# Another order of work on ScalarE and VectorE around three norms and the PLE gate of an encoder layer

## Chip, cores and metric

The kernel runs on one core of a Trainium2 chip. The metric is the device time of one launch in microseconds (us); a lower number is better. The engines of the core are TensorE (PE), VectorE (DVE), ScalarE (ACT), GpSimd (POOL) and SyncE (SP, which issues most of the DMAs). Each engine takes its instructions strictly in the order of its program and waits on semaphores for the others.

## What is computed

One inference layer of a streaming encoder, for 512 prompt tokens and 64 sample tokens, handled together as 576 columns. Everything is float32. The parts that matter here:

```python
    merged = (jax.nn.sigmoid(gate_a) * (o_a.reshape(B, L, -1) @ w_branch_attn)
              + jax.nn.sigmoid(gate_r) * (o_r @ w_branch_ret))
    x = x + rmsnorm(merged @ w_out, g_mix_post)
    h = rmsnorm(x, g_ffn_pre)
    f = (jax.nn.silu(h @ w_ffn_gate) * (h @ w_ffn_up)) @ w_ffn_down
    x = x + rmsnorm(f, g_ffn_post)
    x = x + (p @ w_ple_proj) * jax.nn.sigmoid(x @ w_ple_gate)
```

`D_MODEL` is 1024, the FFN is 2816 wide, and the per-layer embedding `p` (PLE) has 256 columns. `rmsnorm` multiplies each token by the inverse root of its mean square over the 1024 features, then each feature by a gain. Attention and retention come earlier and are not touched.

## The kernel before

**Layout.** Activations lie transposed: features on the 128 partitions, tokens along the free axis. A tensor of width 1024 is eight blocks k (`KD` = 8) of 576 columns, and each block is handled as two halves h of 288 columns (`HALF`). So `(c, h)` names output block c of the features and half h of the tokens.

**Products in three passes.** A float32 operand is split into a high part (a copy rounded to fp32r, made by ScalarE) and a low part (the difference, made by VectorE). `triple` issues three matmuls for each input block k: high times high, high weight times low activation, low weight times high activation. So a unit of one `(c, h)` over eight blocks is 24 matmuls (`half_unit`); `several` runs two or four units side by side, k in the outer loop, so that the blocks of the activation may still be arriving. `hooks` and `behind` put small matmuls between them. On ScalarE `hi` splits a weight tile, on VectorE `lo` makes its low part; for the tiles of the last product both are called `gate_operand`. TensorE waits for a weight tile by a count in `lo_ready`.

**A norm.** It runs once for each half. ScalarE squares each block, VectorE adds the squares into `sqacc`. Then `half_sums_of` (TensorE, six narrow matmuls in the profile's records) sums over the partitions, `half_var_of` (VectorE) scales the sums, `half_power` (GpSimd, L2410) takes the power -0.5, and `half_factor` (TensorE, again six) spreads the factor over the partitions into PSUM.

**The first two norms.** After the product "out", norm 1 gives `scale` and `residual` (VectorE, new x in `res`). Its squares (`res_square` on ScalarE, `add_res_square` on VectorE) feed norm 2, whose factor goes into `normed`. `y_high` (ScalarE) and `y_low` (VectorE) split the result for the FFN. Half 0 goes through all this first, then half 1. The 16 units of "ple" (6 matmuls each, `ple_units`) give TensorE other work in the meantime, and `ple_tile` (ScalarE) copies each result out of PSUM. TensorE's order: ple blocks 0 to 5; "ffn" units 0 to 3 of half 0 side by side; ple blocks 6 and 7; ffn units 0 and 1 of half 1; ffn units 2 and 3 of half 1; ffn units 4 and 5. The first ScalarE function of the FFN is `gate_silu` (L1432).

**The FFN** is 19 groups of seven products and three rounds of "down". Its last round comes with norm 3: `down_out` (VectorE, L2216) adds the PSUM result to `wd`, `down_square` (ScalarE) squares it, `add_down_square` (VectorE) adds, and `scale`, `residual`, `y_high` and `y_low` follow as before, this time without a norm of their own. In this round a down unit has 7 input blocks, 21 matmuls. Order on TensorE: blocks 4 to 7 of half 0, then blocks 4 to 7 of half 1; the sums of half 0 stand in the middle of block 4 of half 1.

**The PLE gate.** Units 0 to 3 of "gate" run as four pairs (two for each half), then units 4 to 7 one by one. For each of the 16 results, in the order `Y_ORDER`: ScalarE applies the sigmoid (`gate_out`, L1568, in place 0 of the order the first use of that table here), VectorE multiplies and adds (L2275, L2277) into `yt`, TensorE transposes it back to rows (`y_transposes(n)`, L1095, three matmuls), ScalarE copies it (`y_rows_out`, L1576), and SyncE sends it out: one DMA for half 0, three for half 1, since half 1 holds rows of two output tensors. Result n on VectorE waits for the transposes of result n - 2.

**Lines of the page that recur.** L942, L943 and L944 are the three matmuls of `triple`, L995 the sums, L1003 the factor. L1918 is VectorE's `lo`, L1955 `scale`, L1964 `residual`, L1972 `normed`, L1978 `y_low`, L1991 `add_res_square`, L2224 `add_down_square`, L1899 VectorE's `gate_operand`. L1392 is `ple_tile`, L1386 `y_high`.

## Time and profile before

| | |
|---|---|
| median of 3 runs | 1001.41 us (1001.06 to 1001.5) |
| the profiled execution, its time | 1001.08 us |
| its span, first to last instruction | 999.2 us |
| TensorE busy | 978.2 us, 98% |
| VectorE busy | 632.1 us, 63% |
| ScalarE busy | 397.0 us, 40% |
| GpSimd busy | 85.7 us, 9% |
| mean granted clock of TensorE | 0.996 of full speed |

All times below are microseconds from the start of the span. A busy share is a mean over the whole span; the stretches around the norms have to be read by themselves. A timeline row gives start, duration, engine, line, operation, output and inputs, and in brackets how long the engine had been idle and what ended that.

### The profile page before, as it was taken

The page shows a single profiled execution, that of the slowest core. Times are in us where ns is not written, and L with a number is a line of the kernel's source. Part 1 is how long each engine was busy: PE and PEld are TensorE (multiplying, and loading weights), DVE is VectorE, ACT ScalarE, POOL GpSimd, SP SyncE. Part 2 cuts the span into 40 slices and gives each one's busy share as a digit, 9 for nine tenths or more (in the row PEclk, how much of TensorE's full clock was granted, in tenths as well). Part 3 has the DMA queues.
Part 4 walks back from the last instruction along what each step waited for, and adds up shares of the span by engine and source line. Part 5 has one row for each costly group of instructions (what it writes and reads, how often), then busy time and mean ns, then how long its engine had stood idle before and what let it go on. Part 6 is the DMA issues. An engine that isn't in the chain of part 4 may idle for free.

```text
span 999.2 us, 19155 instructions
## 1 busy us (share of the span) xinstructions
PE 978.2 (98%) x7256; PEld 954.8 (96%) x7256; DVE 632.1 (63%) x1244; ACT 397.0 (40%) x693; POOL 85.7 (9%) x140
## 2 busy tenths in 40 slices
PE   6999999999999999999998999999999999999997
PEld 5999999999999999999998999999999999999997
DVE  5555666757665634345466899625996469965762
ACT  5324434434343422223454555424453135533252
POOL 1032212212100000010011100000000000030000
PEclk9999999999999999999999999999999999999999
DMA  8434222122222222246512623521334223274211
GB/s 210 126 111 131 82 69 58 58 73 64 62 65 64 84 86 76 82 131 193 151 31 59 228 78 92 148 64 45 110 95 133 64 72 98 81 249 136 85 47 50
DMA packets 166198, 98.45 MB, mean 99 GB/s; under 512 B 14657, under 2 KB 162529, under 8 KB 165873
## 3 DMA queue, kind: packets, MB, share of 16 engines
q1 hardware_dynamic: 159904, 79.19, 28.0%
q0 software_dynamic: 4336, 16.67, 4.7%
q10 hardware_dynamic: 1888, 1.64, 0.6%
q8 instruction: 47, 0.77, 0.3%
q14 instruction: 23, 0.18, 0.1%
HBM read 86.79 MB, written 10.75 MB: 98 GB/s over the span
## 4 chain that ended last, share of the span: by engine, by line
PE 91%; DVE 4%; issue 2%; ACT 2%; DMA 0%; DVEq 0%; SPq 0%; ACTq 0%
PE acc L679 35%; PE acc L942 10%; PE acc L943 10%; PE acc L944 10%; PE small L942 6%; PE small L943 6%; PE small L944 6%; PE small L811 1%; PE small L828 1%; PE small L857 1%; PE small L861 1%; PE small L759 1%; PE small L859 1%; PE small L1095 1%; ACT prob L1183 1%
## 5 line engine op out<-in xcount | busy, mean ns | idle before, releaser
L679 PE MATMUL acc<-xh,whi 128*128 128x288 f32 x736 | 163.1, 303 | 1.6 <-DVE wlo L1606 1.5
L679 PE MATMUL acc<-xh,wlo 128*128 128x288 f32 x736 | 157.3, 295 | 0.0
L679 PE MATMUL acc<-xl,whi 128*128 128x288 f32 x736 | 157.2, 295 | 0.0
L1123 ACT ACTIVATE whi<-raw 128x1024 fp32r<-128x1024 f32 (+1 forms) x62 | 62.1, 1001 | 198.3 <-PE acc L679 198.3
L1606 DVE TENSOR_TENSOR wlo<-raw,whi 128x1024 fp32r<-128x1024 f32 (+1 forms) x64 | 74.2, 1160 | 81.1 <-ACT whi L1123 77.7
L679 PEld LDWEIGHTS acc<-xh,whi 128*128 128x128 f32 x736 | 116.9, 189 | 6.1 <-issue 5.0
L679 PEld LDWEIGHTS acc<-xl,whi 128*128 128x128 f32 x736 | 118.1, 188 | 0.0
L679 PEld LDWEIGHTS acc<-xh,wlo 128*128 128x128 f32 x736 | 118.0, 188 | 0.0
L1918 DVE TENSOR_TENSOR wlo<-raw,whi 128x512 fp32r<-128x512 f32 (+2 forms) x93 | 80.9, 871 | 51.1 <-ACT whi L1334 35.4
L942 PE MATMUL acc<-yh,whi 128*128 128x288 f32 x360 | 107.3, 298 | 1.3 <-DVE wlo L1918 1.3
L944 PE MATMUL acc<-yh,wlo 128*128 128x288 f32 x360 | 106.1, 295 | 0.0
L942 PE MATMUL acc<-fh,whi 128*128 128x288 f32 x264 | 78.3, 297 | 0.0
L944 PE MATMUL acc<-fh,wlo 128*128 128x288 f32 x264 | 78.3, 297 | 0.0
L943 PE MATMUL acc<-fl,whi 128*128 128x288 f32 x264 | 78.3, 296 | 0.0
L943 PE MATMUL acc<-yl,whi 128*128 128x288 f32 x264 | 77.7, 294 | 0.0
L1342 ACT ACTIVATE whi<-s_sum 128x512 fp32r<-128x512 f32 x76 | 47.7, 630 | 61.5 <-DVE s_sum L2100 51.4
L942 PEld LDWEIGHTS acc<-yh,whi 128*128 128x128 f32 x360 | 67.6, 188 | 1.7 <-DVE wlo L1918 1.5
L944 PEld LDWEIGHTS acc<-yh,wlo 128*128 128x128 f32 x360 | 67.6, 188 | 0.0
L1918 DVE TENSOR_TENSOR wlo<-s_sum,whi 128x512 fp32r<-128x512 f32 x76 | 51.6, 682 | 8.6 <-ACT whi L1342 8.6
L1334 ACT ACTIVATE whi<-raw 128x1024 fp32r<-128x1024 f32 (+1 forms) x38 | 38.4, 1012 | 39.6 <-PE acc L944 18.5
L944 PEld LDWEIGHTS acc<-fh,wlo 128*128 128x128 f32 x264 | 50.0, 189 | 0.0
L942 PEld LDWEIGHTS acc<-fh,whi 128*128 128x128 f32 x264 | 50.0, 189 | 0.0
(312 smaller groups left out, 2353.8 us busy)
## 6 DMA issues: line engine op xcount, KB each, us to landing
raw<-in_w_in SPq DMA_DIRECT2D x92, 256.0 KB, 3.1
raw<-in_w_ffn_gate SPq DMA_DIRECT2D x44, 256.0 KB, 3.3
raw<-in_w_ffn_up SPq DMA_DIRECT2D x44, 256.0 KB, 4.0
raw<-in_w_ffn_down SPq DMA_DIRECT2D x32, 256.0 KB, 3.5
res<-x_scratch POOLq DMA_DIRECT2D x16, 288.0 KB, 3.8
raw<-in_w_branch_ret SPq DMA_DIRECT2D x16, 256.0 KB, 3.1
raw<-in_w_out SPq DMA_DIRECT2D x16, 256.0 KB, 4.0
raw<-in_w_ffn_down SPq DMA_DIRECT2D x16, 192.0 KB, 3.7
```

The lines of the kernel that those rows point to most:

```text
L679: ins = nc.tensor.matmul(acc[:, a, hf, 0:HALF], w[:, s, at:at + P], x(k)[:, hf * HALF:(hf + 1) * HALF], start=first and n == 0 and m == 0, ...
L759: ins = nc.tensor.transpose(small[:, at + r * P:at + r * P + size], src[0:size, r, col:col + P], ident[0:size, 0:size])
L811: ins = nc.tensor.matmul(att[0:nq, slot * KW + k0:slot * KW + k1], q_st[64 * g:64 * g + 64, 2 * p + j, 0:nq], k_st[64 * g:64 * g + 64, k0: ...
L828: ins = nc.tensor.matmul(att[64 * g:64 * g + 64, 0:2 * nq], v_st[0:nk, t, 64 * g:64 * g + 64], prob_t[0:nk, t, 2 * g * nq:2 * (g + 1) * nq ...
L942: nc.tensor.matmul(bank, w_h, x_h, start=first, stop=False)
L943: nc.tensor.matmul(bank, w_h, x_l, start=False, stop=False)
L944: return nc.tensor.matmul(bank, w_l, x_h, start=False, stop=last)
L1123: nc.scalar.activation(whi[:, s, 0:n], raw[:, s, 0:n], ACT.Copy).then_inc(hi_ready, 1)
L1334: nc.scalar.activation(dst[:, 0:n], raw_of(RAW[u])[:, 0:n], ACT.Copy).then_inc(hi_ready, 1)
L1342: nc.scalar.activation(dst[:, 0:QUART], s_sum[:, S_STEP[u[2]], :], ACT.Copy).then_inc(hi_ready, 1)
L1606: nc.vector.tensor_tensor(wlo[:, s, 0:n], raw[:, s, 0:n], whi[:, s, 0:n].bitcast(F32), ALU.subtract).then_inc(lo_ready, 1)
L1918: nc.vector.tensor_tensor(dst[:, 0:n], src[:, 0:n], high[:, 0:n], ALU.subtract).then_inc(lo_ready, 1)
```

## The change

It has four parts.

- Norms 1 and 2. On VectorE, `lo` of the ffn weight tiles 1, 2 and 3 moves up, ahead of the loop of `normed` for half 0. On ScalarE the copies `y_high` of half 0 alternate with `ple_tile` from an earlier place on; the eight `res_square` of half 1 follow without `ple_tile` between them; the four `ple_tile` of blocks 6 and 7 move behind `gate_silu(0, 0)`; and a one-element Silu ahead of the squares asks for the table. On TensorE, the sums of half 1 move from behind ple unit (7, 0) to a hook after input block 6 of ffn units 0 to 3, and the factor moves from behind (7, 1) to behind (6, 0).
- Norm 3. `gate_operand(2)` goes behind the last square of half 0 on ScalarE and behind `half_var_of(0, 2)` on VectorE; `gate_operand(3)` goes behind `down_square(4, 1)` and behind `half_var_of(1, 2)`.
- The gate. A one-element Sigmoid on ScalarE stands ahead of the copies `y_high` of half 1. The transposes of results 0 to 3 move from hooks 5 (third pair) and 1, 3, 5 (fourth pair) to hooks 1, 3, 5, 7 of the fourth pair.
- The last two units of the gate are exchanged: (7, 1) runs before (7, 0).

```diff
--- before.py
+++ after.py
@@ -187,7 +187,7 @@
         c0 = KD * g
         order += both("down", range(c0, c0 + KD)) if g < 2 else \
             both("down", range(c0, c0 + 4)) + split("down", range(c0 + 4, c0 + KD))
-    return order + split("gate", range(4)) + both("gate", range(4, KD))
+    return order + split("gate", range(4)) + both("gate", range(4, KD - 1)) + [("gate", KD - 1, 1), ("gate", KD - 1, 0)]
 
 
 def use_order():
@@ -1023,7 +1023,7 @@
             pe.wait_ge(pl_ready, KP)
             behind = {(1, 1): lambda: half_sums_of(0, (sqr_added, 7)), (2, 1): lambda: half_sums_of(1, (sq_added, 14)),
                       (3, 0): lambda: half_factor(0, 1), (4, 1): lambda: half_factor(1, 0),
-                      (7, 0): lambda: half_sums_of(1, (sqr_added, 14)), (7, 1): lambda: half_factor(1, 1)}
+                      (6, 0): lambda: half_factor(1, 1)}
 
             def ple_units(cs):
 
@@ -1040,7 +1040,8 @@
                             behind[(c, h)]()
 
             ple_units(range(PLE_FIRST))
-            several("ffn", [(n, 0) for n in range(4)], yh, yl, ready=lambda k: pe.wait_ge(y_lo, k + 1))
+            several("ffn", [(n, 0) for n in range(4)], yh, yl, ready=lambda k: pe.wait_ge(y_lo, k + 1),
+                    hooks={6: lambda: half_sums_of(1, (sqr_added, 14))})
             ple_units(range(PLE_FIRST, KD))
             several("ffn", ((0, 1), (1, 1)), yh, yl, ready=lambda k: pe.wait_ge(y_lo, KD + k + 1))
             several("ffn", ((2, 1), (3, 1)), yh, yl)
@@ -1099,16 +1100,14 @@
             several("gate", ((0, 0), (1, 0)), yh, yl, ready=lambda k: pe.wait_ge(y_lo, 2 * KD + k + 1),
                     hooks={5: lambda: half_sums_of(1, (sq_added, 28))})
             several("gate", ((2, 0), (3, 0)), yh, yl, hooks={0: lambda: half_factor(1, 2)})
-            several("gate", ((0, 1), (1, 1)), yh, yl, ready=lambda k: pe.wait_ge(y_lo, 3 * KD + k + 1),
-                    hooks={5: lambda: y_transposes(0)})
-            several("gate", ((2, 1), (3, 1)), yh, yl, hooks={1: lambda: y_transposes(1), 3: lambda: y_transposes(2),
-                                                             5: lambda: y_transposes(3)})
+            several("gate", ((0, 1), (1, 1)), yh, yl, ready=lambda k: pe.wait_ge(y_lo, 3 * KD + k + 1))
+            several("gate", ((2, 1), (3, 1)), yh, yl, hooks={1: lambda: y_transposes(0), 3: lambda: y_transposes(1),
+                                                             5: lambda: y_transposes(2), 7: lambda: y_transposes(3)})
             half_unit("gate", 4, 0, yh, yl, hooks={1: lambda: y_transposes(4), 4: lambda: y_transposes(5)})
             half_unit("gate", 4, 1, yh, yl, hooks={1: lambda: y_transposes(6), 3: lambda: y_transposes(7),
                                                    5: lambda: y_transposes(8)})
-            for c in range(5, KD):
-                for h in range(2):
-                    half_unit("gate", c, h, yh, yl, hooks={4: lambda: y_transposes(2 * c + h - 1)})
+            for n in range(10, 2 * KD):
+                half_unit(*Y_ORDER[n], yh, yl, hooks={4: lambda: y_transposes(n - 1)})
             y_transposes(2 * KD - 1)
             assert seen[0] == len(EVENTS)
 
@@ -1405,22 +1404,16 @@
                 res_square(k, 0)
             out_tile(7, 1)
             hi(("ffn", 3))
-            for n in range(10):
+            for n in range(7):
                 ple_tile(n // 2, n % 2)
-            y_high(0, 0, wide, 0, yn_ready)
-            ple_tile(5, 0)
-            y_high(1, 0, wide, 1, yn_ready)
-            ple_tile(5, 1)
-            for k in range(2, KD):
+            for k in range(5):
                 y_high(k, 0, wide, k, yn_ready)
-            for k in range(KD - 2):
+                ple_tile((k + 7) // 2, (k + 7) % 2)
+            for k in range(5, KD):
+                y_high(k, 0, wide, k, yn_ready)
+            nc.scalar.activation(sq_out[:, 0, 0:1], ones[:, 0:1], ACT.Silu)
+            for k in range(KD):
                 res_square(k, 1)
-            ple_tile(6, 0)
-            res_square(KD - 2, 1)
-            ple_tile(6, 1)
-            res_square(KD - 1, 1)
-            ple_tile(7, 0)
-            ple_tile(7, 1)
 
             def gate_silu(i, h):
 
@@ -1443,6 +1436,8 @@
                 nc.scalar.activation(th[:, t], t_full(t), ACT.Copy).then_inc(t_hi, 1)
 
             gate_silu(0, 0)
+            for n in range(2 * PLE_FIRST, 2 * KD):
+                ple_tile(n // 2, n % 2)
             for k in range(6):
                 y_high(k, 1, wide, KD + k, yn_ready)
             f_half(0, 0)
@@ -1543,9 +1538,11 @@
             gate_operand(0)
             for c in range(4, KD):
                 down_square(c, 0)
-                if c < 7:
-                    gate_operand(c - 3)
+                if c == 4:
+                    gate_operand(1)
+            gate_operand(2)
             down_square(4, 1)
+            gate_operand(3)
             y_high(0, 0, res2, 0, res_done)
             y_high(1, 0, res2, 1, res_done)
             down_square(5, 1)
@@ -1557,6 +1554,7 @@
             down_square(7, 1)
             y_high(6, 0, res2, 6, res_done)
             y_high(7, 0, res2, 7, res_done)
+            nc.scalar.activation(sq_out[:, 0, 0:1], ones[:, 0:1], ACT.Sigmoid)
             for k in range(KD):
                 y_high(k, 1, res2, KD + k, res_done)
 
@@ -2006,17 +2004,16 @@
             for k in range(5, KD):
                 add_res_square(k, 0)
             lo(("ffn", 0))
+            lo(("ffn", 1))
             half_var_of(0, 1)
             add_square(7, 1)
-            lo(("ffn", 1))
+            lo(("ffn", 2))
             half_var_of(1, 0)
-            lo(("ffn", 2))
+            lo(("ffn", 3))
             for k in range(KD):
                 normed(k, 0)
                 if k > 0:
                     y_low(k - 1, 0, wide, 0)
-                if k == 3:
-                    lo(("ffn", 3))
             y_low(KD - 1, 0, wide, 0)
             for k in range(KD):
                 scale(k, 1, wide, 0)
@@ -2233,9 +2230,10 @@
             for c in range(4, KD):
                 down_out(c, 0)
                 add_down_square(c, 0)
-                if c < 7:
-                    gate_operand(c - 3)
+                if c == 4:
+                    gate_operand(1)
             half_var_of(0, 2)
+            gate_operand(2)
             down_out(4, 1)
             add_down_square(4, 1)
             dve.wait_ge(back_in, 32 * KD)
@@ -2258,6 +2256,7 @@
             add_down_square(7, 1)
             y_low(KD - 1, 0, res2, 1)
             half_var_of(1, 2)
+            gate_operand(3)
             for k in range(KD):
                 scale(k, 1, wd, 2)
                 if k > 0:
```

## Rows read from the trace of the kernel before

**Rows 1.** Waits of TensorE, whole span: microseconds, times, longest.
```profile
PE small L1095 <- DVE yt L2277: 3.1, 2, 1.6
```

**Rows 2.** Stretches: busy time by engine, granted clock, DMA share.
```profile
528.00:541.00 13.00, 11.72 (x88) 11.49 (x88) 12.27 (x30) 5.94 (x14) 0.00 (x0) 1.00 0.14 42
...
545.00:560.00 15.00, 12.32 (x81) 11.69 (x80) 10.71 (x25) 8.91 (x20) 6.20 (x11) 0.89 0.61 235
...
905.00:930.00 25.00, 23.50 (x169) 23.27 (x169) 14.41 (x27) 8.19 (x13) 0.87 (x1) 0.93 0.28 78
...
950.00:960.00 10.00, 8.43 (x65) 8.19 (x65) 5.79 (x14) 6.03 (x12) 0.00 (x0) 1.00 0.07 16
```

**Rows 3.** Timeline of TensorE around the first two norms: start, duration.
```profile
529.02 0.30 PE L942 MATMUL acc<-yh,whi 128*128 128x288 f32 x1
...
531.64 0.40 PE L942 MATMUL acc<-yh,whi 128*128 128x288 f32 x1 [1.27 <-DVE wlo L1918]
...
543.29 0.29 PE L942 MATMUL small<-ph,whi_p 128*128 128x288 f32 x1
...
546.38 0.67 PE L995 MATMUL small<-ones,sqacc 128*96 128x1 f32 x6 [0.54 <-DVE sqacc L1991]
...
551.00 0.58 PE L942 MATMUL small<-yh,whi 128*128 128x288 f32 x1 [1.87 <-DVE yl L1978]
...
558.99 0.29 PE L942 MATMUL acc<-yh,whi 128*128 128x288 f32 x1
```

**Rows 4.** Timeline of ScalarE there.
```profile
528.42 0.41 ACT L1392 ACTIVATE proj<-acc 128x288 f32<-128x288 f32 x1 [0.72 <-PE acc L944]
...
548.41 1.28 ACT L1432 ACT_TABLE_LOAD   x1
```

**Rows 5.** Timeline of VectorE there.
```profile
523.09 1.21 DVE L1918 TENSOR_TENSOR wlo<-raw,whi 128x1024 fp32r<-128x1024 f32 x1
...
527.73 0.46 DVE L1978 TENSOR_TENSOR yl<-wide,yh 128x288 fp32r<-128x288 f32 x1 [2.24 <-ACT yh L1386]
...
530.37 1.22 DVE L1918 TENSOR_TENSOR wlo<-raw,whi 128x1024 fp32r<-128x1024 f32 x1
...
535.28 0.81 DVE L1955 TENSOR_TENSOR wide<-small,wide 128x288 f32<-128x288 f32 x2
...
543.11 0.44 DVE L1991 TENSOR_TENSOR sqacc<-sqacc,sq_res 128x288 f32<-128x288 f32 x1
```

**Rows 6.** Timeline of GpSimd there.
```profile
523.25 1.76 POOL L2410 TENSOR_TENSOR rstd<-rowvar,neg_half 96x3 f32<-96x3 f32 x1 [1.11 <-DVE rowvar L1948]
...
547.32 0.85 POOL L2410 TENSOR_TENSOR rstd<-rowvar,neg_half 96x3 f32<-96x3 f32 x1 [22.31 <-DVE rowvar L1948]
```

**Rows 7.** Timeline of TensorE at the last norm.
```profile
922.25 0.67 PE L995 MATMUL small<-ones,sqacc 128*96 128x1 f32 x6 [1.50 <-DVE sqacc L2224]
...
926.59 0.38 PE L942 MATMUL acc<-fh,whi 128*128 128x288 f32 x1
```

**Rows 8.** Timeline of VectorE at the last norm.
```profile
920.77 0.45 DVE L2216 TENSOR_TENSOR wd<-small,wd 128x288 f32<-128x288 f32 x1
```

**Rows 9.** Timeline of TensorE at the PLE gate.
```profile
954.72 0.53 PE L1095 MATMUL small<-tab,yt 128*96 128x128 f32 x3 [1.57 <-DVE yt L2277]
...
960.18 0.49 PE L1095 MATMUL small<-tab,yt 128*96 128x128 f32 x3
```

**Rows 10.** Timeline of VectorE at the PLE gate.
```profile
961.65 1.22 DVE L1899 TENSOR_TENSOR wlo<-wlo_raw,whi 128x1024 fp32r<-128x1024 f32 x1
```

**Rows 11.** Timeline of SyncE at the end.
```profile
995.83 0.32 SPq L662 DMA_DIRECT2D out<-y_row  x1
...
996.69 0.52 SPq L665 DMA_DIRECT2D out<-y_row  x1
```

**Rows 12.** DMA issues of the last 8 us: KB each, us to landing.
```profile
out<-y_row SPq DMA_DIRECT2D x1, 144.0 KB, 2.0
...
out<-y_row SPq DMA_DIRECT2D x1, 16.0 KB, 1.6
```

## The prediction

> **What bounds the kernel now.** The table of busy times puts TensorE at the bound, so the only time to win is where it waits or runs slowly. The waits of TensorE show few such places after the start; the longest total there is at the transposes of the gate, 3.1 us in 2 waits [rows 1], of which one belongs to the changed stretch and one to the end. Next I read granted clock by stretch [rows 2]. It is 0.89 over the 15 us around the second norm and 0.93 over the 25 us of the third: worked out between the levels 1.2 and 2.4 GHz, that is 3.3 us and 3.5 us at the lower level, each losing half of itself, 1.65 and 1.75 us. The fall followed an idle of 1.87 us in one place [rows 3] and of 1.50 us plus narrow matmuls in the other [rows 7]. It did not follow the idles of 1.27 us [rows 2, 3] and 1.57 us [rows 2, 9]. Then the timelines of all engines around these waits show who is late, and why.
>
> **Norms 1 and 2, the first stall.** TensorE starts the ffn units at 529.02, and stands 1.27 us until 531.64 for the low part of weight tile 3 [rows 3], which VectorE makes only at 530.37 [rows 5], between the blocks of `normed`. After the change that instruction follows the others directly. VectorE then has three subtractions where it had three before `normed` too: 518.94, 520.08 and 521.68 by my count for tiles 0 to 2, and tile 3 takes the slot at 523.09 that tile 2 has now [rows 5]. `normed` starts no later than before, since it waits for the factor. The stall goes. From 531.64 to 543.29 TensorE issues 87 matmuls, 0.133 us each [rows 3]; unstalled, the 84 ahead of the moved sums bring it from 529.02 to 540.15.
>
> **The moved sums.** They need the last add of the squares of half 1. Now the first low part of half 0 comes at 527.73, after 2.24 us of waiting for ScalarE, whose copy stood behind the tenth ple tile [rows 5]. Ahead of it there will be seven, so it follows `normed` directly, at about 525.6. The following ones go at 0.8 us until ScalarE comes to the twelve tiles' eleventh, which TensorE ends at 528.42 [rows 4]: behind it fifth copy and low part end near 529.6, three more at 0.8, and VectorE reaches the first scale of half 1 at 531.8 and not 535.28 [rows 5]. From 535.28 to the fifth add after the first takes 7.83 us now (543.11) [rows 5], and the two behind it wait for each other, 0.56 and again 0.56 with its own 0.46: 9.4 us in all. So the sum is complete at 531.8 + 9.4 = 541.2, now 546.3, with the sums at 546.38 [rows 3]. TensorE is at the hook at 540.15 and waits 1.1 us. The Silu table, 1.28 us [rows 4], is loaded ahead of the squares, from 531.3, and finds ScalarE idle there: the first residual of half 1 is ready at 533.
>
> **From there to the ffn units of half 1.** Sums 0.53, then 12 matmuls, 6, a factor of 0.59, and 18: the last ple matmul starts at 547.15. The factor isn't late: `half_power` started 0.94 us after the sums and took 0.85 now (546.38 and 547.32) [rows 3, 6], so it ends near 543.0, and TensorE wants it at 544.2. Now 3.35 us lie between the last ple matmul, at 547.65 (sums, 0.53, 6 matmuls), and 551.00; the chain is ple tile, table load, gate Silu, copy, low part. Load and Silu drop out, 1.28 and 0.4 us [rows 4], because the table is there and the Silu stands ahead of the tiles; 1.65 us remain, ScalarE still having to take tile (7, 1) before the copy. The units start at 548.8, 2.2 us earlier. Here TensorE idles 1.5 us. At the upper clock the 48 matmuls take 6.4 us, and VectorE's in-between multiplication of the FFN holds them up 0.4; now they take 558.99 - 551.00 = 7.99 us, slow at first [rows 3]. End 555.55, **3.4 us gained**. VectorE's own chain moves only 2.2 us; the first product's operands lead TensorE by at least 2.7 us by my count in the timeline, so 1.2 us less does no harm.
>
> **Norm 3.** VectorE takes up the last down unit of half 0 only at 920.77 [rows 8], behind three gate operands, each a ScalarE copy and then 1.22 us of subtraction. TensorE ended that unit 15 matmuls before the sums, at 918.6. With two of the operands gone from between, addition, square and add (0.46 each and the steps) give 920.2; TensorE gets to the sums at 920.6 and does not wait 1.50 us until 922.25 [rows 7]. Nor does the clock fall, as I see it. Then sums 0.45 and 12 matmuls: the factor is wanted at 922.7. Here the change adds a wait. `gate_operand(2)` now follows `half_var_of` at once on VectorE, 921.3 to 922.55, and meets `half_power`. Where a subtraction of the same size began at 523.09, the power that began at 523.25 took 1.76 us; with VectorE idle it took 0.85 [rows 5, 6]. The held one ended 0.7 us after the subtraction: here 923.25, 0.55 us too late. I take this one, as the order is the same. Queued behind the factor are all matmuls; `scale` waits for it too. Next matmul 923.85, now 926.59 [rows 7]: **2.7 us gained**, 3.3 without the hold. All behind moves with TensorE; `gate_operand(3)` fits into VectorE's idle time ahead of `scale` of half 1, and the low part is ready 0.5 us before its use by my count.
>
> The Trainium skill, "SBUF — State Buffer", section "Who interferes with whom", says that a VectorE instruction with two SBUF inputs contends with a GpSimd instruction that reads SBUF, and that whoever issues first keeps the shared port for the whole instruction. By that rule the power is held and norm 3 gains 2.7; were the port free it would be 3.3. The 1.76 us of [rows 6] agree.
>
> **The gate.** The transposes of result 0 wait 1.57 us for it, behind load, sigmoid, multiply and add; from the last matmul to the transposes 1.74 us are lost [rows 9]. Moved behind 24 more matmuls they wait for nothing. What is late next: VectorE's result 4 waits for the transposes of result 2, which move from 960.18 [rows 9] to the next hook, 1.92 us on. Its gate operand, now from 961.65, 1.22 us long [rows 10], ends at 964.8, and TensorE wants unit 4 at 964.27 (964.02 now, and the transposes of result 3 ahead). 0.57 us are given back. The results behind it on VectorE are then back to back up to number 8 and just in time. **1.2 us gained.**
>
> **The end.** SyncE issues three DMAs for half 1, the last at 996.69 [rows 11], landing 1.6 us later; the one for half 0 goes out where the first does, at 995.83, and lands 2.0 us later [rows 12]. 998.3 against 997.8: **0.5 us gained.**
>
> Sum: 3.4 + 2.7 + 1.2 + 0.5 = 7.8 us. Span 999.2 - 7.8 = 991.4; the profiled execution took 1.9 us more than its span, and at 1001.08 lies 0.3 below the median. From the median: 1001.41 - 7.8 = 993.6.
>
> **The rivals.** *The clock falls in one of the two new idles* (1.1 us with narrow matmuls behind it, and 1.5 us): 1.65 us lost, 0.4 less in the second, where VectorE sets the pace: 995.0, and 996.5 with both. For: the fall at 1.50 us; against: none at 1.27 and 1.57. *The power isn't held:* 993.0. *The products' operands are the new bound:* the lead in the ffn stretch turns into waits there and its 3.4 us are lost: 997.0. Against: no TensorE wait in 320 us behind it. *The tables don't come early:* a dummy that loads nothing. Then the loads stand in front of their first real use; the Silu waits for ffn unit 0 anyway and the sigmoid has 24 more matmuls ahead of its use, so it still gives about 993.6; the gains lie in the order, and a wholly ineffective change would be 1001.4. *Slower:* the moved sums hold TensorE up. It reaches them at 540.15; if the chain of half 0 didn't shorten, and the sum came at 546.3 as now, TensorE would idle 6.2 us, 5.1 more than I count, and fall in clock twice (2.9): 7.8 + 0.2, the whole gain. That is the point of decision; a us or two later still, and the time is 1003.5. Before half 0's chain could stay so long, ScalarE would have to hold its copies behind the tiles, as it does no longer.
>
> **How the numbers follow.** A measurement of this kernel can tell 0.2%, 2 us, from no change. Chances: my forecast 0.41, one fall of the clock 0.34, both 0.08, power not held 0.05, product operands 0.05, no effect 0.04, slower 0.03. The first five are faster: 0.93; same 0.04; slower 0.03. The likeliest alone spans 992.3 (no hold, sums half a us sooner) to 994.5. The range takes in both falls: 992.3 to 996.8.
>
> **What would show it.** No wait for the low weight near 530; a wait of about 1.1 us at the sums near 541, and of 1.5 us for the low part near 547 to 549; only one table load each, at 531 and near 936; a power of 1.8 us near 921.5 and a wait of half a us for it; no wait at the first transposes, and about 0.6 us for a low part at unit 4; granted clock 1.00 at norm 3. Wrong it is if the clock falls elsewhere, or if TensorE stands at a wait that this list doesn't have.

## The result, and the profile after

The changed kernel takes 993.44 us, median of 4 runs (993.12 to 994.11), beside 1001.23 us (1000.45 to 1001.5) of the kernel before in 4 runs: a ratio of 0.9923, 95% interval 0.9911 to 0.9935, so 7.8 us faster. The profiled execution took 993.12 us with a span of 991.5 us. 993.6 us had been forecast, with a span of 991.4.

The waits of TensorE over the whole span (in total, times, longest), of the kernel after:

```profile
PE small L1096 <- DVE yt L2276: 1.5, 1, 1.5
...
PE small L942 <- DVE yl L1976: 1.3, 1, 1.3
PE small L995 <- DVE sqacc L1989: 0.9, 1, 0.9
...
PE small L1003 <- POOL rstd L2409: 0.4, 1, 0.4
PE acc L942 <- DVE wlo L1897: 0.3, 1, 0.3
```

At the transposes of the gate one wait is left of the two of [rows 1], the one at the very end. The other four lines are the waits that the forecast had listed, no other new one, each shorter by 0.13 to 0.24 us: 1.3 for 1.5 us, 0.9 for 1.1, 0.4 for 0.55, 0.3 for 0.57. Most of that is how a wait is counted. The profile counts idle time from the modelled end of the last matmul, 0.29 us behind its start. The forecast counted from the slot of the next one, 0.13 us behind it: a slot is the time from the start of one matmul to the start of the next, 0.13 us at the upper level of the clock and 0.24 us at the lower.

Windows of the kernel after, with the columns of [rows 2] and at the same times:

```profile
528.00:541.00 13.00, 12.10 (x94) 11.86 (x93) 11.77 (x30) 7.17 (x16) 0.00 (x0) 1.00 0.06 15
...
545.00:560.00 15.00, 13.57 (x101) 13.11 (x100) 11.93 (x23) 7.83 (x17) 2.70 (x6) 1.00 0.71 279
...
905.00:930.00 25.00, 24.58 (x188) 24.35 (x188) 18.04 (x40) 9.76 (x19) 1.79 (x1) 1.00 0.32 96
...
950.00:960.00 10.00, 9.67 (x76) 9.40 (x74) 7.80 (x14) 7.90 (x14) 0.00 (x0) 1.00 0.27 70
```

TensorE's granted clock is 1.00 in all four, where [rows 2] have 0.89 at the second norm and 0.93 at the third: both falls are gone, and no new one came. TensorE issues 101 matmuls and not 81 in the second stretch, 188 and not 169 in the third.

The timeline of TensorE at the first two norms and at the third (start, duration):

```profile
540.54 0.67 PE L995 MATMUL small<-ones,sqacc 128*96 128x1 f32 x6 [0.90 <-DVE sqacc L1989]
...
543.54 0.80 PE L1003 MATMUL small<-tab,rstd 96*128 96x96 f32 x6
...
548.09 0.40 PE L942 MATMUL small<-yh,whi 128*128 128x288 f32 x1 [1.32 <-DVE yl L1976]
...
554.90 0.29 PE L942 MATMUL acc<-yh,whi 128*128 128x288 f32 x1
...
916.51 0.59 PE L995 MATMUL small<-ones,sqacc 128*96 128x1 f32 x6
...
919.22 0.91 PE L1003 MATMUL small<-tab,rstd 96*128 96x96 f32 x6 [0.42 <-POOL rstd L2409]
919.91 0.38 PE L942 MATMUL acc<-fh,whi 128*128 128x288 f32 x1
...
956.07 0.40 PE L942 MATMUL acc<-yh,whi 128*128 128x288 f32 x1 [0.33 <-DVE wlo L1897]
```

The wait near 531 of [rows 3] is gone; the sums go at 540.54 and not at 546.38, and the first matmul of the FFN's half 1 at 548.09 takes 0.40 us where it took 0.58 behind 1.87 us of idle. The 48 matmuls to 554.90 need 6.81 us and not 7.99. At norm 3 the sums do not wait, and 3.40 us behind them comes the first matmul of the next half.

VectorE, with the chain that the sums wait for, and then its wait for ScalarE's first copy of half 1:

```profile
524.89 0.46 DVE L1976 TENSOR_TENSOR yl<-wide,yh 128x288 fp32r<-128x288 f32 x1
...
528.52 0.46 DVE L1976 TENSOR_TENSOR yl<-wide,yh 128x288 fp32r<-128x288 f32 x1 [0.36 <-ACT yh L1385]
...
531.09 0.81 DVE L1953 TENSOR_TENSOR wide<-small,wide 128x288 f32<-128x288 f32 x2
...
538.91 1.58 DVE L1989 TENSOR_TENSOR sqacc<-sqacc,sq_res 128x288 f32<-128x288 f32 x3
...
547.57 0.46 DVE L1976 TENSOR_TENSOR yl<-wide,yh 128x288 fp32r<-128x288 f32 x1 [2.25 <-ACT yh L1385]
```

The first scale of half 1 comes at 531.09 and not at 535.28 [rows 5]. The three last adds, 1.58 us in all, end at 540.49; TensorE starts 0.05 us later.

### The profile page after: what moved, and what is told of

Its sections match the earlier page's. It is cut to its first block, busy times and chain, and to the rows that moved or that the text cites. A ratio compares the mean times of both kernels' runs of the same rounds, so it can differ in the third digit from the quotient of the medians.

```text
span 991.5 us, 19157 instructions
## 1 busy us (share of the span) xinstructions
PE 974.4 (98%) x7256; PEld 951.2 (96%) x7256; DVE 632.0 (64%) x1244; ACT 396.9 (40%) x695; POOL 88.3 (9%) x140
## 4 chain that ended last, share of the span: by engine, by line
PE 92%; DVE 4%; issue 2%; ACT 1%; DMA 0%; POOL 0%; DVEq 0%; ACTq 0%
PE acc L679 35%; PE acc L942 11%; PE acc L943 11%; PE acc L944 11%; PE small L942 6%; PE small L943 6%; PE small L944 6%; PE small L811 1%; PE small L828 1%; PE small L857 1%; PE small L861 1%; PE small L859 1%; PE small L759 1%; ACT prob L1182 1%; PE small L869 1%
## 5 line engine op out<-in xcount | busy, mean ns | idle before, releaser
L679 PE MATMUL acc<-xh,whi 128*128 128x288 f32 x736 | 163.3, 303 | 1.6 <-DVE wlo L1604 1.5
L679 PE MATMUL acc<-xl,whi 128*128 128x288 f32 x736 | 157.0, 294 | 0.0
L679 PE MATMUL acc<-xh,wlo 128*128 128x288 f32 x736 | 156.9, 294 | 0.0
L679 PEld LDWEIGHTS acc<-xh,whi 128*128 128x128 f32 x736 | 116.8, 189 | 6.2 <-issue 5.0
L679 PEld LDWEIGHTS acc<-xl,whi 128*128 128x128 f32 x736 | 118.1, 188 | 0.0
L679 PEld LDWEIGHTS acc<-xh,wlo 128*128 128x128 f32 x736 | 117.7, 188 | 0.0
L1635 DVE TENSOR_TENSOR zt<-acc,rb 128x576 f32<-128x576 f32 x40 | 30.2, 756 | 31.1 <-PE acc L679 31.1
L943 PEld LDWEIGHTS acc<-yl,whi 128*128 128x128 f32 x264 | 49.6, 188 | 0.0
```

What stands on the lines that cost most here:

```text
L679: ins = nc.tensor.matmul(acc[:, a, hf, 0:HALF], w[:, s, at:at + P], x(k)[:, hf * HALF:(hf + 1) * HALF], start=first and n == 0 and m == 0, ...
L943: nc.tensor.matmul(bank, w_h, x_l, start=False, stop=False)
L1635: nc.vector.tensor_tensor(halves(dst), acc_of(a), halves(rb[:, :]), ALU.mult).then_inc(acc_free[a], 1)
```

## Where the time came from

The trace of after stands 0.68 us ahead of the one of before when TensorE starts the ffn units (528.34 against 529.02 [rows 3]). A lead is there ahead of every edit: the same matmul of the first products (L679), behind five transposes of the input (L759), starts at 22.45 and not at 23.26. Over all the profiles of this study the ffn units start between 528.07 and 530.45, so each execution begins a little differently. So I measure stretches of TensorE from one point to the next, and not times from the start:

| Stretch of TensorE | before | after | gained | forecast |
|---|---|---|---|---|
| first ffn matmul to the 48th behind the start of half 1 | 29.97 | 26.56 | 3.41 | 3.4 |
| sums of norm 3, where TensorE gets to them, to the next half's first matmul | 6.00 | 3.40 | 2.60 | 2.7 |
| first matmul behind the factor of half 1 to gate unit 4 | 21.45 | 20.18 | 1.27 | 1.2 |
| last transposes to the end of the span | 4.45 | 4.61 | -0.16 | 0.5 |
| start of the ffn units | 529.02 | 528.34 | 0.68 | not forecast |

(before: 558.99 - 529.02; 926.59 - 920.59, the slot behind the last matmul ahead of the sums, which starts at 920.46; 964.02 - 942.57, where 942.57 is the first matmul behind the factor of half 1. After: 554.90 - 528.34; 919.91 - 916.51; 956.07 - 935.89.) With -0.1 us scattered over the rest the rows make 7.7 us, the difference of the spans, 999.2 - 991.5. Two of these rows may be chance: the end came out against the forecast in this one execution, and the head, which the change doesn't touch, made it up. What each edit earned is a matter for kernels that make one alone.

## Experiments

Each ratio is against the kernel before, timed on the same chip.

### One part at a time

The first four start from the kernel before and make one part of the change each.

**Norms 1 and 2 alone**: the low parts of the FFN's weights, ScalarE's order of ple tiles and copies with the Silu dummy, and TensorE's sums and factor, of which only the last is shown:

```
-                      (7, 0): lambda: half_sums_of(1, (sqr_added, 14)), (7, 1): lambda: half_factor(1, 1)}
+                      (6, 0): lambda: half_factor(1, 1)}
...
+                    hooks={6: lambda: half_sums_of(1, (sqr_added, 14))})
```

> The kernel before with only the part at norms 1 and 2. Theory of the ledger: this stretch, read as the distance from the first ffn matmul to the one behind the ffn pair of half 1, shrinks from 30.0 us to 26.6, the rest stays: 3.4 us gained, 997.8. Norm 3 keeps its 1.5 us wait and its fall of the clock. Rival, the two falls of the clock hang together: what is ahead of norm 3 decides whether it falls there, and the gain is 1.8 or 5 us instead. Rival, this part earns nothing by itself because the products behind it take the lead back: below 1 us.

Measured: 995.26 us (995.02 to 997.38), ratio 0.9957 (0.9944 to 0.9971). The stretch of norms 1 and 2 takes 26.55 us (528.20 to 554.75), so its 3.42 us need nothing of the other parts. But the kernel gained 5.1 us of the 1000.36 beside it, and its norm 3 shows why. TensorE there, in this kernel:

```profile
918.02 0.67 PE L995 MATMUL small<-ones,sqacc 128*96 128x1 f32 x6 [1.50 <-DVE sqacc L2220]
...
920.23 0.80 PE L1003 MATMUL small<-tab,rstd 96*128 96x96 f32 x6
920.82 0.38 PE L942 MATMUL acc<-fh,whi 128*128 128x288 f32 x1
```

It waits the same 1.50 us as in [rows 7], but the next half's first matmul follows 2.80 us behind the sums and not 4.34 us. The stretch from 905 to 930 us in this kernel, and in the one with only the low parts moved (below), which idles 1.52 us there; of that one also TensorE's timeline, with the matmul at which the slots go from 0.13 to 0.24 us:

```profile
905.00:930.00 25.00, 23.50 (x180) 23.26 (x180) 18.43 (x37) 9.37 (x18) 0.87 (x1) 1.00 0.29 87
```

```profile
905.00:930.00 25.00, 23.48 (x168) 23.25 (x168) 15.39 (x29) 9.00 (x15) 0.88 (x1) 0.93 0.27 77
```

```profile
920.42 0.67 PE L995 MATMUL small<-ones,sqacc 128*96 128x1 f32 x6 [1.52 <-DVE sqacc L2223]
...
921.57 0.33 PE L943 MATMUL acc<-fl,whi 128*128 128x288 f32 x1
921.70 0.44 PE L944 MATMUL acc<-fh,wlo 128*128 128x288 f32 x1
921.93 0.45 PE L942 MATMUL acc<-fh,whi 128*128 128x288 f32 x1
922.17 0.45 PE L943 MATMUL acc<-fl,whi 128*128 128x288 f32 x1
...
924.51 0.59 PE L942 MATMUL acc<-fh,whi 128*128 128x288 f32 x1
```

1.00 and 0.93: an idle of the same length was followed by the lower level in one and not in the other. In the second the level drops 1.2 us behind the idle and holds past the factor, 4.09 us from sums to next matmul. The rival of the forecast, that the two falls hang together, fits every trace: the four with a fall at norm 3 (before, the gate, the exchange and the low parts alone) have one at norm 2 as well, and this one has neither. No run separates the two, so it stays a rival. The whole stretch of norm 3 takes 4.46 us here, 1.54 less than in before, and 3.42 + 1.54 is 5.0 us.

The five runs of this kernel lie at 995.0 to 995.3 (three) and 997.1 to 997.4 (two), and only one has a trace. A fall in some of them would explain 1.3 to 1.5 of the 2 us. The random start of an execution can do it without any fall: the kernel without the two one-element activations (below) has spans from 990.2 to 992.7 us at a mean granted clock of 0.999 to 1.0. Which of the two it was here isn't shown.

**Norm 3 alone.**

```
                 add_down_square(c, 0)
-                if c < 7:
-                    gate_operand(c - 3)
+                if c == 4:
+                    gate_operand(1)
             half_var_of(0, 2)
+            gate_operand(2)
...
             half_var_of(1, 2)
+            gate_operand(3)
```

(and ScalarE's copies in the same order)

> The kernel before with only the gate operands of norm 3 moved. Ledger: no wait for the squares, no fall of the clock, a power of about 1.8 us that holds the factor back by 0.4 to 0.6 us: 2.6 us gained, 998.6. Rival: a different place in time lets the clock fall all the same at the short wait for the power, then 1.0 us gained.

Measured: 998.26 us (997.05 to 999.16), 0.9977 (0.9967 to 0.9987). Sums to next matmul 3.40 us (920.46 to 923.86), the factor waits 0.42 us, and the stretch of norms 1 and 2 stays at 29.95 us. Clock 1.00 at norm 3, 0.97 from 500 to 560 us, where before has 0.97 too. The medians give 2.1 us, the stretch 2.6, which is as near as such medians can tell.

**The gate alone**: `y_transposes(0)` to `(3)` at the hooks 1, 3, 5, 7 of units (2, 1) and (3, 1), and the Sigmoid dummy.

```
-            several("gate", ((2, 1), (3, 1)), yh, yl, hooks={1: lambda: y_transposes(1), 3: lambda: y_transposes(2),
-                                                             5: lambda: y_transposes(3)})
+            several("gate", ((2, 1), (3, 1)), yh, yl, hooks={1: lambda: y_transposes(0), 3: lambda: y_transposes(1),
+                                                             5: lambda: y_transposes(2), 7: lambda: y_transposes(3)})
```

> The kernel before with only the moved transposes of the gate and the early Sigmoid. Ledger: 1.74 us of lost TensorE time at the first transposes gone, 0.4 to 0.6 us given back before gate unit 4 for its low part: 1.2 to 1.3 us gained, 1000.0. Rival: the give-back is as large as the gain, 1001.2.

Measured: 999.93 us (997.85 to 1000.89, 11 runs), 0.9995 (0.9986 to 1.0004). The wait at the first transposes is gone and unit 4 waits 0.33 us; factor to unit 4 takes 20.17 us and not 21.45, which is 1.28 us. The time itself can't tell 1.28 us from nothing.

**The exchange of the last two gate halves alone** (with the loop over the last units).

```
-    return order + split("gate", range(4)) + both("gate", range(4, KD))
+    return order + split("gate", range(4)) + both("gate", range(4, KD - 1)) + [("gate", KD - 1, 1), ("gate", KD - 1, 0)]
```

> The kernel before with only the last two gate units exchanged. The step as predicted: one DMA in place of three, 0.5 us gained between the last row copy and the end of the span (3.4 us now). Rival from the trace of the changed kernel: its single 144 KB DMA landed after 2.9 us, so nothing is gained or 0.2 us lost. A third: 2.9 us was one slow landing, and the next run shows 2.0.

Measured: 1000.35 us (998.67 to 1002.01, 11 runs), 0.9996 (0.9987 to 1.0006), again within what can be told. The end in the trace (TensorE's last transposes, SyncE's last issue):

```profile
994.46 0.53 PE L1095 MATMUL small<-tab,yt 128*96 128x128 f32 x3 [1.49 <-DVE yt L2276]
```

```profile
995.54 0.33 SPq L658 DMA_DIRECT2D out<-y_row  x1
```

From the last transposes to the end of the span, 998.2, it is 3.74 us, where before has 4.45: 0.7 gained.

The four stretches add up: 3.4 + 2.6 + 1.3 + 0.7 = 8.0 us. No part needs another. But they overlap: in its one trace the part at norms 1 and 2 brings 1.54 of the 2.6 us at norm 3 with it, since the clock doesn't fall there.

### One part taken away or changed

The next four start from the kernel after.

**Without the two one-element activations**, so that each table is loaded by its first real use.

```
-            nc.scalar.activation(sq_out[:, 0, 0:1], ones[:, 0:1], ACT.Silu)
...
-            nc.scalar.activation(sq_out[:, 0, 0:1], ones[:, 0:1], ACT.Sigmoid)
```

> The changed kernel without the two one-element activations; all else as changed. My rival of the prediction priced the early tables at nothing: the Silu load then stands before the gate Silu near 541.8 and is over by 543.1, ahead of the ple tile at 543.7; the Sigmoid load stands behind the last copy near 945.2, and the first result is ready near 948.4, ahead of its transposes at 949.5. So 993.4 as the changed kernel. Other theory: the tables are worth 1.28 us each where TensorE then waits, 994.7 to 996.

Measured: 992.21 us (991.76 to 994.62), 0.9923 (0.9909 to 0.9937), the same as after. ScalarE in this kernel:

```profile
539.22 1.28 ACT L1424 ACT_TABLE_LOAD   x1
541.48 0.41 ACT L1424 ACTIVATE tb<-acc 128x288 f32<-128x288 f32 x1 [0.98 <-PE acc L944]
...
944.99 1.28 ACT L1564 ACT_TABLE_LOAD   x1
946.28 0.71 ACT L1564 ACTIVATE tb<-small 128x288 f32<-128x288 f32 x2
```

The Silu's table is loaded behind the last square, from 539.22, and the Silu then waits 0.98 us more for TensorE: the load is hidden anyway. The Sigmoid's load stands in front of its use at 946.28, and VectorE is done with the first result at 947.68, 1.5 us ahead of its transposes at 949.17. The stretches of norms 1 and 2 and of the gate take 26.53 and 20.17 us, as in after. Asking early is worth nothing here; the gain stands without it. What is left of the change on ScalarE there is the Silu's place ahead of the ple tiles, which no kernel tests by itself.

**Without the exchange** (and with the old loop over the last units).

```
-both("gate", range(4, KD - 1)) + [("gate", KD - 1, 1), ("gate", KD - 1, 0)]
+both("gate", range(4, KD))
```

> The changed kernel with the last two gate units in their old order. If the exchange loses as its trace says, the end (last row copy to end of span) is 3.4 us as before and this is 0.2 us faster than the changed kernel; if the 2.9 us landing was chance, this one is 0.5 us slower.

Measured: 993.62 us (992.4 to 995.02), 0.9927 (0.9913 to 0.9941). The end takes 4.41 us. The span of 993.4 comes from a late head: the ffn units start at 530.45. Of eight profiles with the exchange seven have 3.69 to 3.78 us at the end and one, that of after, 4.61; of six without it five have 4.39 to 4.45 and one 5.57. So the exchange is worth 0.67 us. One execution of each kind took 0.9 to 1.2 us more, for two different reasons. In the kernel with norm 3 alone it was an issue on SyncE, the one ahead of the last, 1.54 us long where the five others of that kind take 0.45; the last DMA then landed in its usual 1.8 us:

```profile
993.47 1.54 SPq L664 DMA_DIRECT2D out<-y_row  x1
```

In after it was a late landing; DMA issues of its last 8 us (KB each, us to landing):

```profile
out<-y_row SPq DMA_DIRECT2D x1, 144.0 KB, 2.9
```

2.9 us against the 2.0 of [rows 12]; all seven others with the exchange have the wait of 1.6 us for it, this one 2.5.

**The gate operand out of the power's way**: on VectorE `gate_operand(2)` goes behind the next down unit's addition.

```
             half_var_of(0, 2)
-            gate_operand(2)
             down_out(4, 1)
             add_down_square(4, 1)
+            gate_operand(2)
```

> The changed kernel, but VectorE makes the low part of gate tile 2 behind the add of squares (4, 1) and not at once behind the variance of half 0, so it has nothing running when GpSimd takes the power. Port theory: the power takes 0.85 to 0.9 us in place of 1.79, the factor's wait of 0.42 us is gone, 0.4 us gained (993.0), norm stretch 2.6 to 3.0. Rival: the power is long for a reason of its own (DMA descriptors, its place after the reloads) and stays 1.8 us. The low part fits into VectorE's idle time before down unit (5, 1); if not, scale starts up to 1 us later with no cost to TensorE.

Measured: 992.34 us (992.03 to 992.63), 0.9918 (0.9904 to 0.9932). GpSimd in after and in this kernel:

```profile
917.38 1.79 POOL L2409 TENSOR_TENSOR rstd<-rowvar,neg_half 96x3 f32<-96x3 f32 x1 [27.05 <-DVE rowvar L1946]
933.25 1.77 POOL L2409 TENSOR_TENSOR rstd<-rowvar,neg_half 96x3 f32<-96x3 f32 x1 [14.08 <-DVE rowvar L1946]
```

```profile
917.83 0.88 POOL L2409 TENSOR_TENSOR rstd<-rowvar,neg_half 96x3 f32<-96x3 f32 x1 [27.02 <-DVE rowvar L1946]
933.18 1.76 POOL L2409 TENSOR_TENSOR rstd<-rowvar,neg_half 96x3 f32<-96x3 f32 x1 [14.48 <-DVE rowvar L1946]
```

The power of half 0 falls from 1.79 to 0.88 us as soon as no subtraction of 128x1024 stands beside it; that of half 1, which still has `gate_operand(3)` behind its variance, keeps 1.76. The factor no longer waits, and sums to next matmul is 2.71 us, not 3.40: 0.69 us gained. Of these, 0.16 us are given back, against the forecast of no cost to TensorE: the subtraction now stands ahead of `scale` on VectorE, the last add of the squares of half 1 ends at 932.19, and TensorE, which would be at the sums at 932.08, starts them at 932.24. From the first matmul behind the factor to these sums it is 12.57 us here and 12.41 in after:

```profile
932.24 0.67 PE L995 MATMUL small<-ones,sqacc 128*96 128x1 f32 x6
```

This is what the Trainium skill states in "SBUF — State Buffer", section "Who interferes with whom": a VectorE instruction with two SBUF inputs contends with a GpSimd instruction that reads SBUF, the shared ports are an exclusive lock, and the order of issue decides who blocks. The trace agrees: in after the subtraction runs from 917.22 for 1.21 us, to 918.43, and the power ends 0.74 us behind that, at 919.17; left free it takes 0.88 us. The first power of these norms is less clear. In before it starts at 521.13, ahead of a subtraction at 521.35, and takes 1.01 us; in after it starts at 520.73, ahead of one at 520.93, and takes 2.14 us all the same. In both, VectorE's add of squares (two SBUF inputs, 0.45 us) had begun 0.16 us before the power. Why the outcomes differ isn't shown; TensorE waits for neither.

**ScalarE's last tiles and first copies taken in turns**: one ple tile, then copy, tile, copy, tile, copy, tile.

```
-            for n in range(2 * PLE_FIRST, 2 * KD):
-                ple_tile(n // 2, n % 2)
-            for k in range(6):
+            ple_tile(PLE_FIRST, 0)
+            for k in range(3):
+                y_high(k, 1, wide, KD + k, yn_ready)
+                ple_tile((2 * PLE_FIRST + 1 + k) // 2, (1 + k) % 2)
+            for k in range(3, 6):
```

> The changed kernel, but ScalarE copies the first three blocks of half 1 between the last ple tiles and not behind them. Theory: the wait of 1.32 us ahead of the ffn units of half 1 is ScalarE's order, behind tile (7, 1); the first copy can go when normed is done near 544.9, so the wait vanishes and the 0.4 us in the middle too: 1.7 us gained, 991.7. Rival: the first low part is paced by the norm's chain itself, and only a part, under 0.5 us, comes.

Measured: 992.78 us (990.78 to 993.41), 0.9922 (0.9908 to 0.9936), profiled span 989.2. The stretch takes 25.02 us (528.43 to 553.45), 1.54 less than in after. TensorE in this kernel:

```profile
547.46 0.37 PE L942 MATMUL small<-yh,whi 128*128 128x288 f32 x1 [0.19 <-ACT proj L1391]
```

So the wait of 1.32 us at 548.09 was ScalarE's copy standing behind tile (7, 1), as the forecast had it, and nothing in VectorE. What is left is 0.19 us for a tile that frees a PSUM buffer. The median gains less than the trace; its runs lie apart by 2.6 us, and I can't say more of it than that.

### What is left in the stalls

The last four: the low parts alone, from the kernel before, and three steps on from after.

**Only the low parts of `("ffn", 1)` to `("ffn", 3)` moved on VectorE.**

```
             lo(("ffn", 0))
+            lo(("ffn", 1))
             half_var_of(0, 1)
             add_square(7, 1)
-            lo(("ffn", 1))
+            lo(("ffn", 2))
             half_var_of(1, 0)
-            lo(("ffn", 2))
+            lo(("ffn", 3))
...
-                if k == 3:
-                    lo(("ffn", 3))
```

> The kernel before with one piece of the part at norms 1 and 2: VectorE makes the low parts of ffn weight tiles 1 to 3 ahead of normed; ScalarE's and TensorE's orders as before. Theory: the 1.27 us wait near 531 goes, but ScalarE still copies half 0 behind ten ple tiles and squares half 1 between the last tiles, and the sums stay behind unit (7, 0). The chain of half 1 moves by the 1.14 us of one subtraction, so the stretch is 28.5 to 29 us (29.97 before, 26.6 in the whole part): 1 to 1.4 us gained. Rival: the removed wait comes back whole at the sums, 0 gained. Second rival: it is the main thing, 2.5 us or more.

Measured: 999.74 us (998.49 to 1001.0, 11 runs), 0.9993 (0.9984 to 1.0002). TensorE in this kernel:

```profile
544.53 0.67 PE L995 MATMUL small<-ones,sqacc 128*96 128x1 f32 x6 [0.54 <-DVE sqacc L1991]
...
549.15 0.40 PE L942 MATMUL small<-yh,whi 128*128 128x288 f32 x1 [1.87 <-DVE yl L1978]
```

The medians, 1.0 us apart, can't tell this gain from nothing; the stretch can. The wait near 531 is gone, and it takes 28.41 us, 1.56 less than before; the sums wait 0.54 and the ffn units 1.87 us as in [rows 3]. From the start of the ffn units to that of half 1 it is 20.43 us here, 21.98 before and 19.75 in after; the 48 matmuls behind take 7.98, 7.99 and 6.81 us. So of the 3.4 us of norms 1 and 2, 1.55 are the late low part, 0.7 the moved sums with ScalarE's order, and 1.2 the clock, which still falls behind the 1.87 us (0.97 from 500 to 560 us, as before) and no longer behind 1.32.

**The gate's transposes one hook earlier**, at 0, 2, 4, 6.

```
-hooks={1: lambda: y_transposes(0), 3: lambda: y_transposes(1), 5: lambda: y_transposes(2), 7: lambda: y_transposes(3)})
+hooks={0: lambda: y_transposes(0), 2: lambda: y_transposes(1), 4: lambda: y_transposes(2), 6: lambda: y_transposes(3)})
```

> The changed kernel with the transposes of results 0 to 3 at hooks 0, 2, 4, 6 of the fourth gate pair in place of 1, 3, 5, 7. Theory: VectorE's result 4, its gate operand and with it unit 4 come 0.8 us earlier relative to TensorE, the wait of 0.33 us for a low part at unit 4 vanishes and the gate stretch shrinks by 0.4 to 0.6 us (slow restart included). Rival: result 0 isn't ready at hook 0 and the wait comes back there; its second addition ended 2.4 us before hook 1, so it should be ready.

Measured: 992.94 us (992.33 to 994.35), 0.9922 (0.9909 to 0.9936). Unit 4 waits for nothing. From the factor to the fifth transposes (the first in unit 4) it is 20.47 us, in after 21.08: 0.61 gained, the wait of 0.33 us and the slow start behind it. The give-back of the gate was thus the transposes' place, as argued.

**The sums one hook later, with the turns of ScalarE.**

```
-                      (6, 0): lambda: half_factor(1, 1)}
+                      (6, 1): lambda: half_factor(1, 1)}
...
-                    hooks={6: lambda: half_sums_of(1, (sqr_added, 14))})
+                    hooks={7: lambda: half_sums_of(1, (sqr_added, 14))})
```

> The interleaved kernel with the sums of half 1 one input block later (hook 7) and the factor behind ple unit (6, 1). Theory: the wait of 0.90 us for the last add of squares is gone, as the sums come at about 541.2 from a first ffn matmul at 528.4; the factor is then just ready, and the copies have two ple units, 1.6 us, of cover: stretch 24.1 to 24.6 us (25.0 interleaved). Rival: what is won at the sums is lost as a wait of 0.8 us for the first low part, since the chain from the squares to the low part is the bound of this stretch: stretch 25.0.

Measured: 990.9 us (990.58 to 993.01, 4 runs), 0.9908 (0.9893 to 0.9923). TensorE in this kernel:

```profile
541.27 0.59 PE L995 MATMUL small<-ones,sqacc 128*96 128x1 f32 x6
...
543.39 0.81 PE L1003 MATMUL small<-tab,rstd 96*128 96x96 f32 x6
...
545.58 0.40 PE L942 MATMUL small<-ph,whi_p 128*128 128x288 f32 x1 [0.56 <-ACT proj L1391]
...
547.24 0.37 PE L942 MATMUL small<-yh,whi 128*128 128x288 f32 x1 [0.20 <-ACT proj L1391]
```

The wait at the sums is gone, and 0.56 us of it comes back at a ple unit, whose PSUM buffer ScalarE's tile hasn't freed, now that a copy stands in between. The stretch is 24.71 us, 0.31 less than with the turns alone: neither the whole 0.9 nor nothing, but a wait handed on to ScalarE.

**All four together**: turns, late sums, early hooks, operand out of the way.

> The changed kernel with all four: copies between the last ple tiles, sums one block later, low part of gate tile 2 behind the add, transposes one hook earlier. If the stretches add: 1.5 + 0.5 + 0.7 + 0.5 = 3.2 us faster than the changed kernel, so 3.2 + 7.8 = 11.0 us faster than before, ratio 0.989. If they eat each other, 2.2 us.

Measured: 990.41 us (989.81 to 992.05, 4 runs), 0.9902 (0.9887 to 0.9917), with a profiled span of 988.2. Stretches: 24.73; 2.72; factor to fifth transposes 20.48; end 3.75. The waits of TensorE in this kernel:

```profile
PE small L1096 <- DVE yt L2278: 1.5, 1, 1.5
...
PE small L942 <- ACT proj L1391: 0.8, 2, 0.6
```

10.3 us faster than the kernel before on the same chip, and 3.0 us under the median of after. The stretches add, as forecast: against after 1.83, 0.68 and 0.60 us, less the 0.16 us given back behind norm 3 (12.57 us here too).

## Why the prediction was right

**Norms 1 and 2, 3.4 us: right, with its steps.** Taken 0.68 us later, as the head was early, the trace of after says first low part 525.57 (forecast 525.6), first scale of half 1 531.77 (531.8), sums 541.22 (541.2), ffn units of half 1 548.77 (548.8), end of the stretch 555.58 (555.55). The last ple matmul starts at 547.15, as forecast. The low parts alone give 1.55 us of the term, more than the 1.27 of the wait: the profile counts a wait 0.16 us short (0.29 against 0.13), and the slot of the matmul behind it is 0.24 us and not 0.13; the kernel with the turns shows what the rest still waits for.

**Norm 3, 2.7 us: 2.6.** The power is held (1.79 us) and the factor waits 0.42 us. That the hold comes from the operand put behind the variance was only argued from [rows 5, 6]; moving that operand away showed it, with 0.69 us against the 0.6 that the forecast gave between its two cases, of which 0.53 last to the sums of half 1.

**The clock: right in the outcome, and weaker as a reason.** The two new idles, 0.90 us at the sums and 1.32 us at the ffn units, had together a chance of 0.42 of a fall. Six kernels' profiles have both idles (after, norms 1 and 2 alone, without tables, without the exchange, operand away, early hooks), and in all six the clock is 1.00 from 500 to 560 us. But "the fall followed an idle of 1.50 us" can't be read as a rule of length: that idle was followed by the lower level in before, in the gate, exchange and low-part kernels, and not in the kernel with norms 1 and 2 alone. So the forecast had the outcome of both norms right, but its reason, the length of the idle, doesn't carry norm 3 by itself. In before the fall is there; with norms 1 and 2 changed alone it was already gone. What else decides it stays open.

**The gate, 1.2 us: 1.3.** Transposes wait for nothing, unit 4 for 0.33 us. The give-back was put at 0.57 us; the early hooks take it away and gain 0.61. The trace shows a wait of only 0.33, and the same two additions as above, 0.16 us of counting and 0.11 us of slow slot, make it 0.60.

**The end, 0.5 us: mis-sized, 0.67 measured.** The term gave the last DMA of half 1, issued at 996.69 on line 665, the landing of 1.6 us in [rows 12]. That row is the DMA of 16 KB, which line 664 issues before it. The last one carries 32 KB; DMA issues of the last 8 us of the kernel before:

```profile
out<-y_row SPq DMA_DIRECT2D x1, 32.0 KB, 1.8
```

996.69 + 1.8 is 998.5, against 995.83 + 2.0 = 997.8 with the exchange: 0.7 us and not 0.5. The rest of the end is the same for both: the span ends 0.7 us behind the landing, at 999.2 in before and at 998.2 in the kernel with the exchange alone, whose DMA lands at 995.54 + 2.0 = 997.5. In the profile of after a landing of 2.9 us hid the gain.

**The rivals.** A fall in the new idles did not come, the products' operands made no wait of TensorE, the sums did not hold it for more than 0.9 us. That the tables don't come early: they do (one load each, from 530.70 and 932.01), and it makes no difference, as this rival said.

With the end at 0.67 the sum is 8.0 us; the medians differ by 7.8. The interval of the ratio is 1.2 us wide to either side, so the medians can't tell 7.8 from 8.0, and that the forecast met the median to 0.2 us is partly luck. What supports it is that each stretch came out as forecast, to 0.2 us.

## What to carry to other kernels

Ask what stands in front of the one instruction that is waited for: here it was never the work itself but its place behind tiles or low parts in an in-order queue, and a stall that was taken away came back smaller at the next queue. Measure edits of one us by the stretch between two points of the bound engine within one trace, because the time of the whole kernel carries a random head (2.4 us between these profiles) and a random end (once a late landing, once a long issue). An instruction of 96x3 elements on GpSimd doubled in time beside a long two-input subtraction of VectorE, so keep the one that TensorE waits for clear of it.

## What the runs showed that was not expected

- After an idle of 1.50 to 1.52 us at the same place TensorE's granted clock fell in four profiles (0.93 over 905 to 930 us) and not in a fifth (1.00), though the same matmuls lie on both sides of it. A fall costs 1.3 to 1.5 us (4.09 and 4.34 against 2.80 us from sums to next matmul).
- A table load of 1.28 us costs nothing where ScalarE waits for data, and the activation behind it starts within 0.01 us of its end (530.70 + 1.28, then 531.99).
- The landing of the last store, counted from the start of its issue, is 2.0 us in seven of eight profiles with the exchange and 2.9 us in one, which sets the end of the span. In one profile without it an issue on SyncE took 1.54 us where the five others take 0.45.
- A power on GpSimd (96x3) that began 0.2 us ahead of a subtraction on VectorE (128x1024) took 1.01 us in before and 2.14 us in after.
